# Four rows of layer 2's output product beside its last attention head, and pieces of queries that end with a slot

## The reference

```python
n = rms_norm(h, mix_norm_g)
z = n @ w_in
a, gate, c_q, c_kv, k_r = split(z)
u = a * sigmoid(gate)                                   # convolution branch, 512 wide
u = causal_depthwise_conv(u, conv_w, conv_b)            # 31 taps
u = silu(layer_norm_2(u, conv_ln_g, conv_ln_b))
q  = rms_norm(c_q, q_norm_g) @ w_uq                     # 8 heads of 64 + 32 (rotated)
kv = rms_norm(c_kv, kv_norm_g) @ w_ukv
o = block_causal_attention(qf, kf, v, chunk_id)         # 8 heads
mix = concatenate([rms_norm(u, conv_out_g), rms_norm(o, attn_out_g)])
h = h + mix @ w_out                                     # 1024 x 1024
```

## Time and profile before

| | |
|---|---|
| three runs | 3750.66, 3755.87, 3758.26 us (median 3755.87) |
| the profiled execution, device time | 3758.68 us |
| its span, first to last instruction | 3756.9 us |
| mean granted clock of TensorE | 0.965 of full |
| TensorE busy | 3503.6 us, 93% |
| weight loads busy | 2817.5 us, 75% |
| VectorE, ScalarE, GpSimd busy | 1758.4 (47%), 1121.7 (30%), 1074.6 us (29%) |
| chain that ended last | TensorE 80%, VectorE 12%, ScalarE 5%, issue 2%, DMA 1% |
| layer 2's attention (160 slots) | about 1540 to 1861 us of the span |

### The profile page before, as it was taken

One profiled execution on the slowest core, in us unless ns is written; L12 is line 12 of the kernel. 1 busy time (PEld: TensorE's weight loads), 2 busy tenths in 40 slices (PEclk: granted clock), 3 DMA queues, 4 the chain that ended last, 5 costly groups with the idle time before them and its releaser, 6 DMA issues.

```text
span 3756.9 us, 39301 instructions
## 1 busy us (share of the span) xinstructions
PE 3503.6 (93%) x16304; PEld 2817.5 (75%) x16304; DVE 1758.4 (47%) x1820; ACT 1121.7 (30%) x1491; POOL 1074.6 (29%) x1144
## 2 busy tenths in 40 slices
PE   9988889999999999998889999999989999999997
PEld 6655667888887688555588988998966777777776
DVE  4566553222223578576455544644654223443422
ACT  3333243111112432444531111111334322322432
POOL 3111344232233333100023433433422222211243
PEclk9999999999999999899999999999999999999999
DMA  3000211111111121000111111111121111100232
GB/s 119 23 28 23 95 62 56 51 45 51 45 46 51 63 90 34 17 6 6 52 46 40 46 45 47 45 50 45 46 84 40 62 62 40 32 25 29 73 129 95
DMA packets 56250, 192.23 MB, mean 51 GB/s; under 512 B 6900, under 2 KB 7284, under 8 KB 55560
## 3 DMA queue, kind: packets, MB, share of 16 engines
q1 hardware_dynamic: 56072, 189.71, 14.8%
HBM read 172.83 MB, written 16.86 MB: 50 GB/s over the span
## 4 chain that ended last, share of the span: by engine, by line
PE 80%; DVE 12%; ACT 5%; issue 2%; DMA 1%; POOL 0%; ACTq 0%; SPq 0%; DVEq 0%; POOLq 0%
PE psum L263 21%; PE psum L265 21%; PE psum L264 21%; PE psum L136 13%; DVE work L96 3%; DVE mix L105 2%; DVE res L96 2%; PE psum L296 1%; PE psum L298 1%; PE psum L297 1%; DVE res L105 1%; ACT L124 1%; ACT res L124 1%; DVE u_padded L96 1%; DVE work L114 1%
## 5 line engine op out<-in xcount | busy, mean ns | idle before, releaser
L96 POOL TENSOR_TENSOR w_lo<-w_raw,w_hi 128x256 fp32r<-128x256 f32 x1140 | 1074.4, 973 | 2647.3 <-ACT w_hi L129 2647.1
L263 PE MATMUL psum<-x_hi,w_hi 128*128 128x512 f32 (+2 forms) x3336 | 1258.3, 377 | 36.2 <-DVE mix L96 7.2
L264 PE MATMUL psum<-x_lo,w_hi 128*128 128x512 f32 (+2 forms) x3336 | 1210.3, 363 | 0.0
L265 PE MATMUL psum<-x_hi,w_lo 128*128 128x512 f32 (+2 forms) x3336 | 1208.0, 362 | 0.0
L129 ACT CAST w_hi<-w_raw 128x1024 fp32r<-128x1024 f32 x285 | 298.2, 1048 | 1635.0 <-PE psum L265 1538.8
L263 PEld LDWEIGHTS psum<-x_hi,w_hi 128*128 128x128 f32 x3336 | 634.8, 190 | 148.6 <-issue 40.8
L264 PEld LDWEIGHTS psum<-x_lo,w_hi 128*128 128x128 f32 x3336 | 635.7, 191 | 93.6 <-issue 20.6
L265 PEld LDWEIGHTS psum<-x_hi,w_lo 128*128 128x128 f32 x3336 | 633.3, 190 | 81.1
L263 PE MATMUL psum<-h_hi,w_hi 128*128 128x512 f32 x848 | 338.4, 399 | 15.5 <-issue 9.0
L265 PE MATMUL psum<-h_hi,w_lo 128*128 128x512 f32 x848 | 336.1, 396 | 0.0
L264 PE MATMUL psum<-h_lo,w_hi 128*128 128x512 f32 x848 | 333.6, 393 | 0.0
(11 more groups left out here) (281 smaller groups left out, 3586.3 us busy)
## 6 DMA issues: line engine op xcount, KB each, us to landing
w_raw<-w_dram SPq DMA_DIRECT2D x285, 512.0 KB, 3.3
res<-spill SPq DMA_DIRECT2D x4, 1044.0 KB, 8.2
res<-x_dram SPq DMA_DIRECT2D x8, 512.0 KB, 8.3
res<-x_dram SPq DMA_DIRECT2D x4, 1024.0 KB, 8.2
spill<-res SPq DMA_DIRECT2D x1, 4096.0 KB, 12.1
spill_a<-mix SPq DMA_DIRECT2D x8, 512.0 KB, 2.6
res<-spill_a SPq DMA_DIRECT2D x8, 512.0 KB, 4.7
x_plain<-spill SPq DMA_DIRECT2D x4, 1024.0 KB, 10.3
```

What stands on the lines that cost most here:

```text
L96: self.mark(self.e.tensor_tensor(out, a, b, op), inc)
L263: t.e.matmul(out, whi, xhi, start=k == 0, stop=False, skip_group_check=True)
L264: t.e.matmul(out, whi, xlo, start=False, stop=False, skip_group_check=True)
L265: ins = t.e.matmul(out, wlo, xhi, start=False, stop=last_k, skip_group_check=True)
```

## The change

- `pe_next_head` splits the fill by slots: keys two steps a slot for three slots (one piece each), queries two steps and one step in turn, so that each piece of queries ends with a slot. Even heads need slots 0 to 8, odd ones 0 to 5.
- In the last head, `pe_last` takes the place of the fill: rows 0 to 3 of "uo", three steps a slot, all on banks 0 to 2 (`claim_three`), 48 steps in slots 140 to 155. ScalarE copies each finished row to `M[m]` (after all low parts of the branch rows exist, since these are read from there).
- The branch is spread over 122 slots instead of 140 (step 61+j falls into slot ceil(122 j / 91) − 1: step 124 in slot 84 instead of 96, step 152 in 121 instead of 139), and its rows are rounded in slots 130, 132, 134 and 136.
- After the last slot only rows 4 to 7 of "uo" are left. VectorE adds `M[0]` to `M[3]` to the residual from SBUF, in the same place of its queue as before.

```diff
--- before.py
+++ after.py
@@ -243,9 +243,9 @@
     def view(self, p, rows=slice(0, P)):
         return self.ps[rows, p.first:p.first + p.width, 0:p.cols]
 
-    def product(self, t, key, chunks, hi, lo, pieces, ready, parts=1):
-
-        p, before = self.claim(key, len(pieces), pieces[0][1], parts)
+    def product(self, t, key, chunks, hi, lo, pieces, ready, parts=1, claimed=None):
+
+        p, before = claimed or self.claim(key, len(pieces), pieces[0][1], parts)
         block0 = len(self.blocks)
         self.blocks += chunks
         for stream, value in before:
@@ -285,6 +285,19 @@
         before.append((self.slots[0], self.slot_uses[0]))
         self.slot_uses[0] += parts
         p = Product(key, bank, 1, cols, self.slots[0], self.slot_uses[0])
+        assert key not in self.products, key
+        self.products[key] = p
+        return p, before
+
+    def claim_three(self, key):
+
+        before = []
+        if self.kind != "three":
+            before = [(s, n) for s, n in zip(self.slots, self.slot_uses)]
+            self.kind, self.turn = "three", 0
+        before.append((self.slots[0], self.slot_uses[0]))
+        self.slot_uses[0] += 1
+        p = Product(key, 0, 3, 348, self.slots[0], self.slot_uses[0])
         assert key not in self.products, key
         self.products[key] = p
         return p, before
@@ -1343,7 +1356,9 @@
     SCORE_AT = {10: 3, 11: 8, 12: 2, 13: 7, 14: 1, 15: 6, 16: 4, 17: 5}
     ROW_AT = {17: (0,), 19: (1, 2)}
     SMALL = (0, 4, 8)
-    STEPS, LAST_STEP = 91, 140
+    STEPS, LAST_STEP = 91, 122
+    U_AT = {130: 0, 132: 1, 134: 2, 136: 3}
+    LAST_ROWS, LAST_FILL = 4, 3
 
     def __init__(self, core, ffn):
         self.k, self.ffn, s = core, ffn, core.s
@@ -1605,10 +1620,31 @@
                                                      for b in range(3)], k.hi, k.lo, THREE, lambda b: [(self.p_ready, 3 + b)], 2, bank)
 
     def pe_next_head(self, t, h):
-        if h < H2:
-            if h % 2 == 0:
-                yield from self.pe_keys(t, h // 2, 7)
-            yield from self.pe_queries(t, h, 7)
+
+        if h % 2 == 0:
+            keys = self.pe_keys(t, h // 2, 7)
+            for _ in THREE:
+                advance(keys, 2)
+                yield True
+            drain(keys)
+        queries = self.pe_queries(t, h, 7)
+        for _ in THREE:
+            advance(queries, 2)
+            yield True
+            advance(queries, 1)
+            yield True
+        drain(queries)
+
+    def pe_last(self, t):
+
+        t.wait_ge(self.shifted, 8 * H2)
+        for m in range(self.LAST_ROWS):
+            yield from self.pe_out(t, "uo", 0, m, self.k.claim_three(("uo", m)))
+
+    def pe_out(self, t, name, first, m, claimed=None):
+        k = self.k
+        yield from k.product(t, (name, m), [block_of("w_out_2", first + c, m * P) for c in range(4)], lambda c: k.x_hi[:, first + c, :],
+                             lambda c: k.x_lo[:, first + c, :], THREE, lambda c, i: [(self.m_ready, first + c + 1)], 1, claimed)
 
     def first_key(self, i):
         return META + (i - 1) * P if i else 0
@@ -1757,10 +1793,10 @@
         for c in range(len(CHUNKS2)):
             h, s = divmod(c, A_HEAD)
             if s == 0:
-                fill = self.pe_next_head(t, h + 1)
+                fill = self.pe_next_head(t, h + 1) if h + 1 < H2 else self.pe_last(t)
             if c + 2 < len(CHUNKS2):
                 self.pe_chunk(t, c + 2)
-            advance(fill, 2)
+            advance(fill, 1 if h + 1 < H2 else self.LAST_FILL)
             k.label(("fill", c))
             if h + 1 < H2 and s in self.SCORE_AT:
                 self.pe_score(t, h + 1, self.SCORE_AT[s])
@@ -1776,15 +1812,14 @@
             k.label(("slot", c))
         self.pe_column(t, 3 * H2 - 1)
         self.pe_spread(t, 3 * H2 - 1)
+        drain(fill)
         k.label("mix 2")
         t.wait_ge(self.shifted, 8 * H2)
         for freed in self.ring_freed[-3:]:
             t.wait_ge(*freed)
         for n, first in (("uo", 0), ("oo", 4)):
-            for m in range(8):
-                drain(k.product(t, (n, m), [block_of("w_out_2", first + c, m * P) for c in range(4)],
-                                lambda c: k.x_hi[:, first + c, :], lambda c: k.x_lo[:, first + c, :], THREE,
-                                lambda c, i: [(self.m_ready, first + c + 1)]))
+            for m in range(0 if first else self.LAST_ROWS, 8):
+                drain(self.pe_out(t, n, first, m))
             if n == "uo":
                 self.pe_ones(t, ("o rms",), self.A[3], self.o_total, 3, self.rms_sum)
         k.label("out 2")
@@ -1837,6 +1872,10 @@
             kind, n, i = p.key if len(p.key) == 3 else (*p.key, None)
             k.cast(a, p.tiles)
             a.wait_ge(*p.done)
+            if kind == "uo":
+                a.wait_ge(self.m_ready, 4)
+                a.copy(thirds_of(self.M[n]), k.view(p), inc=p)
+                continue
             cols = None if i is None else slice(THREE[i][0], THREE[i][0] + THREE[i][1])
             bank = k.ps[:, p.first, :]
             if kind == "v2":
@@ -1939,11 +1978,11 @@
             advance(branch, self.taps(c))
             if self.ended(c) is not None:
                 self.act_head_copy(a, c)
-            if c >= self.LAST_STEP + 4 and c % 4 == 0:
-                self.act_u_row(a, (c - self.LAST_STEP) // 4 - 1)
+            if c in self.U_AT:
+                self.act_u_row(a, self.U_AT[c])
             k.cast(a, k.at["slot", c][0])
         drain(branch)
-        k.cast(a, k.at["mix 2"][0])
+        self.act_products(a, "mix 2")
         for c in range(4):
             self.act_o_row(a, c)
         for m in range(8):
@@ -2165,8 +2204,8 @@
                 self.dve_inverse(v, self.ended(c - 2))
             if self.ended(c - 4) is not None:
                 self.dve_head_out(v, self.ended(c - 4))
-            if c >= self.LAST_STEP + 4 and c % 4 == 0:
-                self.dve_u_row(v, (c - self.LAST_STEP) // 4 - 1)
+            if c in self.U_AT:
+                self.dve_u_row(v, self.U_AT[c])
         self.dve_inverse(v, 3 * H2 - 1)
         self.dve_head_out(v, 3 * H2 - 1)
         drain(branch)
@@ -2174,9 +2213,13 @@
             self.dve_o_row(v, c)
         for m in range(8):
             p, x = k.products["uo", m], k.res[:, m, :]
-            v.wait_ge(*p.done)
             v.wait_ge(self.h0_back[m // 2], 48)
-            v.tt(thirds_of(x), thirds_of(x), k.view(p), ALU.add, inc=p)
+            if m < self.LAST_ROWS:
+                v.wait_ge(*p.freed)
+                v.tt(x, x, self.M[m], ALU.add)
+            else:
+                v.wait_ge(*p.done)
+                v.tt(thirds_of(x), thirds_of(x), k.view(p), ALU.add, inc=p)
         self.dve_root(v, ("o rms",), self.A[0], self.A[1], 4, 4 * P)
         for m in range(8):
             p, x = k.products["oo", m], k.res[:, m, :]
```

## The result

The changed kernel takes 3767.89 us (median of 20 runs) against 3757.36 us (20 runs of the kernel before): a ratio of 1.0029, 95% interval 1.0023 to 1.0035, some 11 us slower. The forecast was 9 us slower, 3765 us, and rows 0 to 3 of the product did move beside the last head. The profiled execution is the longest of the 20, 3776.4 us, and 6.3 us of its lateness lie ahead of layer 2's attention, where the change doesn't reach (the first exp of 16x400 at 1548.03 instead of 1541.75). So it is read by stretches, not by its span.

A forecast was written before the change was run, and what follows sets the result against it. TensorE was taken to bound the kernel, with work in flight for 93% of the span. Move +9.6, pieces −8.2 + 2, taps +2.5, norm +3 gave about +9 us: 3765 us against the median, own range 3759 to 3771, with rivals 3749 to 3778.

The forecast's parts named there:

- rows into the last head, with the waits between them: Last head: attention hides nothing of the 48 added steps, +23.8 us, and three waits between rows add +1.7.
- rows out of the tail, with the idle spot and the clock: Tail: four rows leave, −22.9 us; TensorE idles +4.2 before row 6 and the lower clock behind it adds +2.8.
- the move in all: Last head and tail: moving the four rows makes the kernel 9.6 us slower in sum.
- pieces of queries, with slot 8: Attention heads: seven waits of 1.17 us go, −8.2 us; a later rounding at slot 8 of even heads costs +2.
- taps at the faster pace: Score stretches, slots 8 to 16: 7 taps instead of 6 on a nearly full VectorE, +2.5 us (0 to 6).
- the norm moved: Branch norm, slots 98–139 to 85–121: subtract-and-add under scores +6, first root out −5, rest +2; +3 us (−12 to +12).
- Rival 1: Last head has room: 9 of 10 us of the rows vanish, the sum is 0; 3756 us, chance 0.14.
- The waits between rows: Last head: each next row waits for ScalarE to copy the previous one out of banks 0 to 2; +1.7 us (0 to 3).
- don't decide it: Tail: the residual's DMAs are in by 1875.3, so they don't set when row 6's banks come free, at 1878.4.
- 0.6 us a head, four heads: Score stretches: one more tap makes a head 0.9 us longer, less in places; four heads at 0.6, +2.5 us.
- Rival 4: Norm's subtract-and-add steps under scores wait for VectorE's backlog, clock at half behind each: +12 to +15, 3775 us, chance 0.18.
- Rivals 2 and 3: Norm: first root and its lower clock leave the scores, 3747 us, chance 0.12; or mild collisions, norm −6, 3751 us, 0.11.

The follow-up runs named there:

- without the rows: The changed kernel with all eight rows of the first output product left in the tail: 3762.95 us, ratio 1.0016 to the kernel before.
- the pieces alone: The kernel before with only the change's `pe_next_head`, so that query pieces end with a slot; branch and rows as before: 3750.83 us, ratio 0.9984.
- the taps alone: The kernel before with the 63 taps at the change's faster pace and the norm's steps in their old slots: 3764.06 us, ratio 1.0015.
- branch alone: The kernel before with only its branch spread over 122 slots and its rows rounded in slots 130 to 136: 3769.9 us, ratio 1.0033.
- the adds in another order: The changed kernel with VectorE adding rows 4 and 5 of the product ahead of rows 0 to 3: 3767.25 us, ratio 1.0021.
- the rows and the norm out of the scores: Against the kernel with the norm's chains in slots 98 to 107 and 118 to 128: four rows moved, adds of rows 4 and 5 first: 3775.71 us, 1.0044.
- the chains in the fill: The changed kernel, all rows in the tail, with the norm's chains put into slots 98 to 107 and 118 to 128: 3766.38 us, ratio 1.0022.
- the compact form: Kernel before with query pieces ending with a slot, old tap pace, norm chains in slots 98–106 and 120–128, odd heads' queries in slots 3–8: 3787.05 us, 1.0083.
- eighteen useless matmuls: The kernel with norm chains in slots 98–107 and 118–128, all rows in the tail, plus 18 unread matmuls each in slots 109 and 129: 3758.6 us, 1.0007.
- ten: Kernel before with query pieces ending with a slot, norm chains in slots 97–108 and 118–128, ten unread matmuls each in slots 109 and 129: 3760.33 us, 1.0009.

## Why the prediction was right, and which steps were not

| step | forecast us | measured us | from |
|---|---|---|---|
| rows into the last head, with the waits between them | +25.5 | +24.3 | last head, with and without the rows |
| rows out of the tail, with the idle spot and the clock | −15.9 | −17.4 | tail, with and without the rows |
| the move in all | +9.6 | +6.9 (trace), +5 (ratios) | without the rows |
| pieces of queries, with slot 8 | −6.2 | −6 | the pieces alone |
| taps at the faster pace | +2.5 | +5.0 (trace), +5.6 (ratio; 2 to 9) | the taps alone |
| the norm moved | +3 | some +7 (1 to 13) | branch alone less taps alone: 0.0018 |
| sum | +9 | 10.9 (ratio of the change) | |

**The move of the rows** was right in its sign and its mechanism. From the exp of chunk 140 to the tail the changed kernel takes 50.74 us and the one without the rows 26.46, so a step costs 24.3 / 48 = 0.506 us beside attention, against 0.478 in the tail; with one visible wait of 0.65 us inside, the two are as good as equal, and the last head hid nothing. Rival 1 is out. With it goes the use that it made of the Trainium skill (Trainium Kernel Development and Optimization, Best Practices), which judges the distance to the roofline by the busy share of LDWEIGHTS: the weight loads were busy 49% of the window of the earlier trace rows, and there was no room for a step. The waits between rows were overrated, 0.65 us visible instead of 1.7. In the tail the adds in front did hold row 6, until 15.46 us after the first row's start (forecast 15.7), but TensorE idled 2.21 us, not 4.2: the clock had already fallen where the tail begins, which made rows 4 and 5 late by 1.7 us (3.42 at 0.50). That fall the prediction doesn't have, and why it comes is open: it is there in the changed kernel and with the adds in another order, not in any kernel without the rows, and not with the rows and the norm out of the scores. The idle spot cost the clock 1.7 us (3.41 at 0.50) instead of 2.8. Together that is 5.6 us, where the tail shrank 5.5 less than 22.9. That the adds cause the idle spot is shown by the other order, which took back 3.4 us in the trace. The prediction's "don't decide it" of the residual's DMAs is right for the order of the change and only for that: with the adds out of the way they hold row 6 next. The four adds took 4.62 us. POOL was idle all that time, so what an add from SBUF costs beside it was not tested.

**The pieces** came out as summed. By head the working was off: it had 1.17 us gained in each and 0.5 to 0.7 given back in three; measured, 1.4 us are gained where the fill is queries alone and 0.7 where it holds keys too.

**The taps** came out at twice their price, though the interval of the ratio just takes in 2.5. The step that failed is "0.6 us a head, four heads": I counted one more tap in the score stretch, and took the first half of a head to be free. It isn't quite: in the changed kernel a new wait of 0.61 us for an inverse of the softmax sums stands in heads 0 and 2. That a tap ahead of it in VectorE's queue causes it is argued from the order of that queue, not tested by itself:

```profile
1640.68 0.64 PE L134 MATMUL psum<-identity,softmax_inverse_columns 128*64 128x128 f32 x4 [0.61 <-DVE softmax_inverse_columns L114]
```

Left out altogether was the clock, which fell twice more with the taps alone; whether the small new waits bring that about isn't shown.

**The norm** is the step that was wrong in more than size. I had priced its place cluster by cluster (+6, −5, +2), mostly by waits. The stretches between the exps of 16x400 and 16x256, each less the same stretch undisturbed, give what the clusters cost where they were and where they went:

| us | subtract-and-add steps into the scores | first root out of them | all the rest, taps included |
|---|---|---|---|
| forecast | +6 | −5 | +2 and some of the 2.5 for taps |
| the change against the pieces alone | +7.0 | −0.8 | +3.5 |
| branch alone against before | +5.3 | −3.8 | +11.5 |

The subtract-and-add steps cost about what was forecast: 14.1 us under the scores (first row, 28.29 against 14.17), after 7.1 in the fill (32.35 against 25.26). The root left the scores and by the first pair gained next to nothing: it had cost 10.0 us under the scores (24.21 us against 14.17), and costs 9.3 in the fill (third row, 34.52 against 25.26). The clusters share their stretches with a few other steps, which are counted with them:

```profile
1724.67:1752.96 28.29, 22.23 (x82) 13.39 (x82) 14.36 (x19) 14.03 (x25) 0.00 (x0) 0.81 0.00 1
...
1736.38 0.85 PE L134 MATMUL psum<-identity,softmax_inverse_columns 128*64 128x128 f32 x3 [2.64 <-DVE softmax_inverse_columns L114]
...
1752.96:1787.48 34.52, 28.69 (x107) 17.75 (x108) 13.73 (x19) 22.69 (x46) 0.00 (x0) 0.81 0.00 0
```

But the two pairs have the same steps in the same slots and put the price in different places, so a cluster has no price of its own that its waits would give. Over the whole stretch the idle time was nearly as large in every arrangement with the whole norm inside (18 to 25 us). What differs more is the time lost to the clock: 14.3 us before, 15.6 with the pieces, 22.7 with the change, 26.6 with the branch alone, 31.0 with the chains in the fill, 37.0 in the compact form. The length less both is 105 to 110 us in all of them, and smallest where most is lost, as it must be if the third number counts too much. Rival 4 named scores that wait for VectorE's backlog as the cause of a large loss. Such a wait is there in the changed kernel (second row, 2.64 us), but the chains in the fill lost more without one. So the sign held, but not for the reason given. What decides whether the clock falls for a few us at a given idle spot, or for a whole score stretch, is open: of my attempts to steer it, moving the chains and the compact form failed, eighteen useless matmuls kept both score stretches up, and ten kept one of two.

Rivals 2 and 3, a norm that gets cheaper, are out with some +7 for it. Of the signs that the prediction named, these came: 29.09 us for the "some 31" in the last head, an idle spot before row 6 with the lower clock behind it, no 1.17 us rows, heads 1 to 3 no longer than before by more than 0.4 us, a last score stretch at 1.00, and 103.8 us for the two heads with most of the norm, not far from 99. Of three waits for a copy one came.

The errors cancel: the move 3 to 5 us too dear, taps and norm some 7 us too cheap. That the total came within 2 us is luck to that extent.

## What to carry to other kernels

Work moved from a tail into a stretch where the same engine is already the bound was paid in full here; look whether a step costs less there than alone, by two stretches that differ only in such steps, before moving it. When adds or copies are put in front of the operation that frees a bank, let the one that frees it go first, even if the others could start sooner, and look when its own operands are there. Split every stretch into work, idle time and time lost to the clock before you explain it: with the branch alone, the chains in the fill and the compact form, most of what the stretch grew by was in the third.

## What the runs showed of the hardware

A continuous stream of attention and score matmuls (f32 chunks of 97 and 128 partitions by 65 to 128 columns of weights, score items of 96 partitions) runs at 1.00 in most undisturbed heads, but the stream itself doesn't hold the clock there. In the kernel with the chains in the fill it began at 1.00 and was at 0.50 from 1765.35 on with TensorE busy 20.93 of 20.93 us; in the compact form it did so in a head without any norm, busy 17.06 of 17.06. The same stretch elsewhere is busy just so at 1.00. Nor does the stream always keep a low clock low: before, behind the 2.48 us idle at the first root, it ran at 0.50 for 6.83 us, busy all the time, and then at 1.00 again.

```profile
1780.38:1787.21 6.83, 6.83 (x21) 3.09 (x20) 6.48 (x8) 1.37 (x5) 0.00 (x0) 0.50 0.00 0
```

The Trainium skill (TensorE: Matmul & The Clock Gate, What's actually happening) says that the clock follows how busy the PE has been; by these traces, busy as the profile shows it doesn't tell the two cases apart. Eighteen dense fp32r matmuls of 128x128 weights and 512 columns right where the clock had fallen, 4.3 us of useless work, kept it at 1.00: done twice, it made the stretch from chunk 80 to 140 10 us shorter with both lots in it. Ten did so in one place and not in the other.
